# A two-block transformer forward pass on one core: PSUM reads of the latent attention moved to ScalarE, broadcast steps on VectorE, and three steps told or split earlier

## The chip, the cores and the metric

The kernel runs on one core of a Trainium2 chip. The metric is device time in microseconds (us); of the kernel before there are three runs.

## The reference, cut to what matters

All arithmetic is float32, 256 tokens of width 2048. A first block (sliding-window attention, gated linear attention, feed-forward, final norm) feeds a second one (convolution, latent attention, attention over 256 memory rows). Nearly all work is the product of activations with weights. What the change touches:

```python
q = (rms_norm(c_q, q_norm_g) @ w_uq).reshape(b, s, 16, 128 + 64)
q_nope = rms_norm(q[..., :128], qn_nope_g)
q_rope = apply_rope(rms_norm(q[..., 128:], qn_rope_g), cos, sin)
kv = (rms_norm(c_kv, kv_norm_g) @ w_ukv).reshape(b, s, 16, 128 + 128)
k_nope = rms_norm(kv[..., :128], kn_nope_g);  v = kv[..., 128:]
k_rope = apply_rope(rms_norm(k_rope_raw, kn_rope_g), cos, sin)
sc = q_nope @ k_nope + q_rope @ k_rope        # per head, masked by chunks of 64
o = softmax(sc * scale) @ v
k, v = split(rms_norm(mem, mem_norm_g) @ w_mem_kv)     # memory rows
x = rms_norm(x, norm_final_g)                # between the blocks; then normed again by block two
```

## The kernel before, in words

TensorE multiplies in float32 by three products: each weight is split into a high part `w_hi` (ScalarE, a copy to float32r, L1064) and a low part `w_lo` (VectorE, raw minus high, L1396); activations likewise. The unit of weights is a **granule**: 512 KB, 1024 columns, 12 matmuls of 128x512 (L437 to L439). SyncE loads granules into 8 raw buffers; the split parts have 4 buffers, so the split of granule g waits for granule g-4 to be used (`w_used`), and TensorE waits for `lo_done`. A **chunk** is a run of granules that fills one of two PSUM accumulators (`acc`); whoever reads it out tells `acc_free`. A **unit** is a small job of TensorE on one of four PSUM banks (transposes L568, scores L914 and L915, read-out L933): TensorE waits for `unit_src`, tells `unit_done`, and the reader tells `unit_free`. VectorE and ScalarE may also ask each other (`act_req`, `act_done`). Each engine runs its own list in the order written; a `Walk` object counts granules, chunks and units on ScalarE and VectorE, and `ahead`, `more`, `some`, `back` say at which place in the list a split stands.

**The latent attention** (16 heads, `mla_pair`, 8 pairs of heads, two loops i of four pr) takes two heads at once. TensorE: chunk `uq` (two granules of 768 columns), chunk `ukv` (two granules), then background chunks, cut into pieces by `MLA_BACK`: in even pairs `mz`, 8 granules, as 3, 2, 2, 1; in odd pairs `gc` and `conv_out`, 12 granules, as 4, 3, 3, 2. Between the pieces stand the pair's units: three of transposes (queries, rope queries, keys), two of scores, two transposing probabilities, one read-out. On VectorE a pair is: read `uq` (L2347) and `ukv` (L2354, L2357) from PSUM, twelve sums of squares (L1410), the reciprocal root by 11 small steps (`rsqrt`, L1416 to L1425), scale per head into `stage` (L2381, L2388, L2398), `rotate` the rope part, read the transposed units (L2403 to L2410), scale, mask and take the maximum of scores (L2422 to L2430), read the transposed probabilities (L2450), scale the read-out (L2463). ScalarE does the exponentials (L1143). The first pair of the first loop (`turn`) also turns half of the convolution. At pr 3 the next pair's four splits are not made ahead.

**The other places.** In four passes of the first block's feed-forward (`ffn_pass` with `mem`) TensorE also transposes a quarter of the raw memory rows behind the second granule of the `up` chunk (`with_turn`); VectorE tells `unit_src` for it at L1959, behind `take_silu`, though the rows lie in SBUF from the start. At the end of the feed-forward `square_parts` (L2050) takes for each of four quarters the sum of squares of x and of x times the gain, six VectorE instructions a quarter; quarters 2 and 3 stand between single splits. For the rope key (L2313 to L2322) VectorE norms and rotates 64 columns while `ckv` is multiplied.

## Time and profile before

| | us |
|---|---|
| three runs | 2757.66, 2759.08, 2759.46 (median 2759.08) |
| the profiled execution | 2757.25, span 2755.5 |
| TensorE busy, of the span | 2604.4 (95%) |
| VectorE busy | 1634.5 (59%) |
| ScalarE busy | 1082.2 (39%) |

The profile is one execution. Times in rows are us from the start of the span; PE is TensorE, DVE VectorE, ACT ScalarE. A bracket in a row of the timeline is the idle time before it and what ended it. "DVEq" is VectorE's queue: an increment of a semaphore, not an instruction's end.

### The profile page before, as it was taken

To read this page: it belongs to the slowest core of one execution; us is meant where nothing else is said; L and a number is where in the kernel's file an instruction comes from. 1 tells how busy PE (TensorE), PEld (TensorE's weight loads), DVE (VectorE), ACT (ScalarE), POOL (GpSimd) and SP (SyncE) were. 2 spreads that over 40 slices of the span, in tenths; PEclk is the share of its full clock that TensorE was granted. 3 is DMA by queue.
4 is the path that set the end of the run, shared out by engine and by line. 5 is a ranking of instruction groups with operands and counts; after the bars stand their busy time and mean duration, and the time that the engine had idled before them with its cause. 6 is when DMAs were issued, how large, how long until landed. Compare 5 with 4: busy or idle time off the path is not lost.

```text
span 2755.5 us, 31202 instructions
## 1 busy us (share of the span) xinstructions
PE 2604.4 (95%) x11745; PEld 2128.5 (77%) x11745; DVE 1634.5 (59%) x2588; ACT 1082.2 (39%) x1309; POOL 0.2 (0%) x4
## 2 busy tenths in 40 slices
PE   5999989999998999999999989899998998999999
PEld 4777667888877788888888768787887777778887
DVE  5565555456655555556556765557666767765454
ACT  3333423444433444433555434333333333334443
POOL 0000000000000000000000000000000000000000
PEclk9999999999999999999999999999999999999999
DMA  5855334655665566665656555455664444446554
GB/s 186 227 161 149 118 120 139 196 176 193 193 195 161 164 187 184 190 190 183 199 183 214 161 153 174 138 162 168 185 183 142 140 141 146 142 129 191 189 185 137
DMA packets 235304, 466.70 MB, mean 169 GB/s; under 512 B 19051, under 2 KB 27537, under 8 KB 234530
## 3 DMA queue, kind: packets, MB, share of 16 engines
q1 hardware_dynamic: 231296, 457.89, 53.3%
q10 hardware_dynamic: 3874, 7.01, 1.3%
q8 instruction: 85, 1.39, 0.2%
q14 instruction: 49, 0.40, 0.0%
HBM read 459.60 MB, written 5.24 MB: 169 GB/s over the span
## 4 chain that ended last, share of the span: by engine, by line
PE 85%; DVE 10%; DMA 2%; ACT 2%; issue 1%; SPq 0%; DVEq 0%; ACTq 0%
PE acc L437 24%; PE acc L439 23%; PE acc L438 23%; DVE w_lo L1396 2%; PE banks L568 2%; PE banks L774 1%; PE banks L773 1%; PE banks L775 1%; DMA bias_rows<-work 1%; PE acc L773 1%; PE acc L774 1%; PE acc L775 1%; ACT w_hi L1064 1%; DMA raw<-in_w_in_dram 1%; DVE etmp L1410 1%
## 5 line engine op out<-in xcount | busy, mean ns | idle before, releaser
L1396 DVE TENSOR_TENSOR w_lo<-raw,w_hi 128x1024 fp32r<-128x1024 f32 (+1 forms) x866 | 1042.9, 1219 | 857.4 <-ACT w_hi L1064 833.7
L1064 ACT ACTIVATE w_hi<-raw 128x1024 fp32r<-128x1024 f32 (+1 forms) x866 | 908.1, 1055 | 1357.8 <-PE acc L439 1220.8
L437 PE MATMUL acc<-w_hi,x_hi_A 128*128 128x512 f32 x1880 | 756.0, 402 | 28.6 <-DVE w_lo L1396 23.5
L438 PE MATMUL acc<-w_lo,x_hi_A 128*128 128x512 f32 x1880 | 741.3, 394 | 0.0
L439 PE MATMUL acc<-w_hi,x_lo_A 128*128 128x512 f32 x1880 | 741.2, 394 | 0.0
L437 PE MATMUL acc<-w_hi,x_hi_B 128*128 128x512 f32 (+1 forms) x1216 | 478.1, 393 | 11.1 <-DVE w_lo L1396 8.4
L438 PE MATMUL acc<-w_lo,x_hi_B 128*128 128x512 f32 (+1 forms) x1216 | 473.6, 389 | 0.0
L439 PE MATMUL acc<-w_hi,x_lo_B 128*128 128x512 f32 (+1 forms) x1216 | 473.5, 389 | 0.0
L437 PEld LDWEIGHTS acc<-w_hi,x_hi_A 128*128 128x128 f32 x1880 | 359.6, 191 | 113.6 <-issue 21.6
L439 PEld LDWEIGHTS acc<-w_hi,x_lo_A 128*128 128x128 f32 x1880 | 358.8, 191 | 77.4
L438 PEld LDWEIGHTS acc<-w_lo,x_hi_A 128*128 128x128 f32 x1880 | 359.9, 191 | 73.2 <-issue 0.8
L437 PEld LDWEIGHTS acc<-w_hi,x_hi_B 128*128 128x128 f32 x1216 | 231.1, 190 | 59.2 <-issue 10.6
L439 PEld LDWEIGHTS acc<-w_hi,x_lo_B 128*128 128x128 f32 x1216 | 230.6, 190 | 46.2
L438 PEld LDWEIGHTS acc<-w_lo,x_hi_B 128*128 128x128 f32 x1216 | 231.1, 190 | 44.4
L568 PE MATMUL banks<-cst,stage 128*128 128x128 f32 (+1 forms) x363 | 59.6, 300 | 66.1 <-DVE stage L1507 19.6
L568 PEld LDWEIGHTS banks<-cst,stage 128*128 128x128 f32 (+1 forms) x363 | 45.4, 152 | 81.0 <-DVE stage L1507 21.6
L773 PE MATMUL acc<-w_hi,x_hi_B 128*128 128x512 f32 x176 | 68.8, 391 | 0.9 <-DVE w_lo L1396 0.9
L775 PE MATMUL acc<-w_hi,x_lo_B 128*128 128x512 f32 x176 | 68.5, 389 | 0.0
L774 PE MATMUL acc<-w_lo,x_hi_B 128*128 128x512 f32 x176 | 68.5, 389 | 0.0
L773 PE MATMUL banks<-w_hi,x_hi_B 128*128 128x512 f32 x176 | 68.5, 389 | 0.0
L774 PE MATMUL banks<-w_lo,x_hi_B 128*128 128x512 f32 x176 | 68.5, 389 | 0.0
L775 PE MATMUL banks<-w_hi,x_lo_B 128*128 128x512 f32 x176 | 68.5, 389 | 0.0
(247 smaller groups left out, 1372.0 us busy)
## 6 DMA issues: line engine op xcount, KB each, us to landing
raw<-in_w_in_dram SPq DMA_DIRECT2D x377, 512.0 KB, 4.0
raw<-in_w_ffn_gate_dram SPq DMA_DIRECT2D x88, 512.0 KB, 4.3
raw<-in_w_ffn_up_dram SPq DMA_DIRECT2D x88, 512.0 KB, 4.4
raw<-in_w_ffn_down_dram SPq DMA_DIRECT2D x88, 512.0 KB, 4.4
raw<-in_w_out_dram SPq DMA_DIRECT2D x32, 512.0 KB, 4.4
raw<-in_w_mem_kv_dram SPq DMA_DIRECT2D x32, 512.0 KB, 4.7
raw<-in_w_mla_out_dram SPq DMA_DIRECT2D x32, 512.0 KB, 4.7
raw<-in_w_o_dram SPq DMA_DIRECT2D x32, 512.0 KB, 3.8
```

The source lines that it names most:

```text
L437: mm(o, xh, hi[:, k, :], start=(kt == first_k), stop=False)
L438: mm(o, xh, lo[:, k, :], start=False, stop=False)
L439: last = mm(o, xl, hi[:, k, :], start=False, stop=(kt == (last_k or c.kts) - 1))
L568: return pe.transpose(o, i, ident[0:i.shape[0], 0:i.shape[0]])
L773: mm(o[q][t], xh, hi, start=first, stop=False)
L774: mm(o[q][t], xh, lo, start=False, stop=False)
L775: ins = mm(o[q][t], xl, hi, start=False, stop=last)
L1064: act.activation(w_hi[:, s, 0:n], raw[:, r, 0:n], ACT.Copy).then_inc(hi_done, 1)
L1396: dve.tensor_tensor(w_lo[:, s, 0:n], raw[:, r, 0:n], w_hi32[:, s, 0:n], ALU.subtract).then_inc(lo_done, 1)
L1410: return dve.tensor_tensor_reduce(out=o, in0=a, in1=b, scale=1.0, scalar=0.0, op0=ALU.mult, op1=ALU.add, accum_out=acc_)
```

## The change

- Latent attention, ScalarE: it reads `uq`, `ukv` (a Square and a Copy of each part that is normed), the three transposed units and the two of probabilities. The split of ScalarE's list around them is as before.
- Latent attention, VectorE: sums of squares become three `tensor_reduce` over ScalarE's squares; the rope rotation is done on unscaled queries, before the first piece of background; the per-head scale becomes one `tensor_tensor` with a broadcast factor for each of three stage buffers; scores are scaled and masked in one step with a mask of three blocks; `rotate` takes both halves of the tokens at once. The order of the units becomes queries, keys, rope queries. Two units wait for `unit_free` (`taken`), since ScalarE now fills what they read.
- The next pair's four splits are made ahead at every pair but the last.
- Memory rows: `unit_src` is told at the head of the pass.
- Squares of quarters 2 and 3: ScalarE squares with a sum, VectorE multiplies the squares by the gain's squares (`fin_sq`, made once, at j = FG + 9) and sums: two instructions a quarter.
- Rope key: `W.more()`, two splits, ahead of it.

```diff
-            def unit(fill):
+            def unit(fill, taken=False):
                 pe.wait_ge(unit_src, U.at(1))
+                if taken:
+                    pe.wait_ge(unit_free, U.at())
...
+            for k in (2, 3):
+                for kt in (4 * k, 4 * k + 2):
+                    split_unit("A", kt, GCOL["norm_final_g"] + kt)
+                for t in range(T):
+                    ins = act.activation(squared[:, k - 2, t, :], xres[:, t, k * CW:(k + 1) * CW], ACT.Square,
+                                         accum_out=sm[:, 4 + 4 * t + k:5 + 4 * t + k])
+                ins.then_inc(squares_done, 1)
+                W.some(1)
...
+            def evac_unit(dst, n, scale=1.0):
+                act.wait_ge(unit_done, W.U.at(1))
+                act.activation(dst, W.bank()[:, 0:n], ACT.Copy, scale=scale).then_inc(unit_free, 1)
...
                 W.background(1 + pr % 2, False, 2)
+                act.wait_ge(w_used, W.E.next(uq.grans))
+                act.activation(q_squares, a[:, :, 0:384], ACT.Square)
+                act.activation(qs, a[:, :, 0:384], ACT.Copy).then_inc(release(uq), 1)
...
                 W.back(ks[0])
+                act.wait_ge(w_used, W.E.next(ukv.grans))
+                act.activation(k_squares, kv4[:, :, :, 0:DN], ACT.Square)
...
                 W.back(ks[1])
-                skip_units(3)
+                for dst, n, g in ((qnT, 512, "mla_qn_nope_g_2"), (knT, 512, "mla_kn_nope_g_2")):
+                    evac_unit(dst.rearrange("p h s -> p (h s)"), n, gcol[:, GCOL[g]:GCOL[g] + 1])
+                evac_unit(qrT, S)
...
-                if pr < 3:
+                if (i, pr) != (1, 3):
                     W.ahead(4)
...
             def ffn_pass(i, first=False, mem=None):
+                if mem is not None:
+                    for p in range(2):
+                        dve.sem_inc(unit_src, 1)
+                        SRC.n += 1
...
+                dve.wait_ge(*released(uq))
+                dve.tensor_reduce(sm[:, 4:8].rearrange(four, t=T), sq4[:, :, :, DN:DN + DR], AX.X, ALU.add)
+                dve.tensor_reduce(sm[:, 0:4].rearrange(four, t=T), sq4[:, :, :, 0:DN], AX.X, ALU.add)
...
+                rotate(rotated, rq, 2)
...
                 W.back(ks[0])
+                dve.wait_ge(*released(ukv))
+                dve.tensor_reduce(sm[:, 8:12].rearrange(four, t=T), k_squares, AX.X, ALU.add).then_inc(step, 1)
...
+                for u, (x, n, o) in enumerate(((q4[:, :, :, 0:DN], DN, 12), (kx, DN, 20), (rotated, DR, 16))):
...
+                    TT(s, x, r, ALU.mult).then_inc(unit_src, 3 if last else 1)
```

**How the order moves.** First place: VectorE, an even pair, from the reciprocal root (its last step) to the transposed units. `stage` is what TensorE transposes, `cs` the cosines, `banks` the units' PSUM. Before:

```order
L1425 SCALAR_TENSOR_TENSOR sm<-sm 128x12 [waits step]
L2381 TENSOR_SCALAR stage<-arena,sm 128x128 [waits step]
L2381 TENSOR_SCALAR stage<-arena,sm 128x128 x3
L2388 SCALAR_TENSOR_TENSOR arena<-arena,sm,rope_g 128x64 [waits unit_src]
L2388 SCALAR_TENSOR_TENSOR arena<-arena,sm,rope_g 128x64 x3
L2276 TENSOR_TENSOR stage<-arena,cs 128x2x32 [waits step]
```

and of the change:

```order
L1472 SCALAR_TENSOR_TENSOR sm<-sm 128x12 [waits step]
L2432 TENSOR_TENSOR stage<-arena,sm 128x512 [waits step]
L2432 TENSOR_TENSOR stage<-arena,sm 128x512 [waits unit_src]
L2432 TENSOR_TENSOR stage<-arena,sm 128x256 [waits unit_src]
L1443 TENSOR_TENSOR w_lo<-raw,w_hi 128x1024 [waits hi_done,unit_src]
L1443 TENSOR_TENSOR w_lo<-raw,w_hi 128x1024 [waits hi_done] x3
```

Behind the root there stood 24 instructions up to the last stage buffer, 12 of them the rotation; now there stand three.

Second place: ScalarE, from the second granule of background to the transposed units, of the change (before, only the L1074 rows were there, as L1064):

```order
L1383 ACTIVATE work<-acc 128x768 [waits w_used]
L1384 ACTIVATE arena<-acc 128x768
L1074 ACTIVATE w_hi<-raw 128x1024 [waits w_used,landed4]
L1074 ACTIVATE w_hi<-raw 128x1024 [waits w_used,landed5]
L1393 ACTIVATE work<-acc 128x512 [waits w_used]
L1394 ACTIVATE arena<-acc 128x512
L1395 ACTIVATE arena<-acc 128x512
L1074 ACTIVATE w_hi<-raw 128x1024 [waits w_used,landed6]
```

Five reads of PSUM now stand among the splits, each waiting for a chunk's end.

Third place: VectorE ahead of the rope key, of the change (before, the L1443 rows were absent here and came behind the rotation):

```order
L1541 SCALAR_TENSOR_TENSOR x_lo_B<-banks,gcol,x_hi_B 128x256
L1443 TENSOR_TENSOR w_lo<-raw,w_hi 128x1024 [waits hi_done,unit_free]
L1443 TENSOR_TENSOR w_lo<-raw,w_hi 128x1024 [waits hi_done]
L1457 ISA etmp,sm<-work 128x64
L1457 ISA sm 128x1
```

Two splits moved ahead of the key's norm. Activation tables are loaded seven times in either listing of ScalarE.

## Rows read from the trace of the kernel before

**Rows 1.** Waits of PE, whole span: us in total, times, longest

```profile
PE acc L437 <- DVE w_lo L1396: 31.9, 16, 4.3
PE banks L568 <- DVEq L1959: 14.6, 4, 3.7
PE banks L568 <- DVEq L2393: 12.9, 8, 2.2
```

**Rows 2.** Timeline of PE, feed-forward passes: start us, us, what

```profile
777.97 1.04 PE L568 MATMUL banks<-cst,stage 128*128 128x128 f32 x8
778.76 0.47 PE L437 MATMUL acc<-w_hi,x_hi_B 128*128 128x512 f32 x1
...
828.77 1.03 PE L568 MATMUL banks<-cst,stage 128*128 128x128 f32 x8
...
982.85 1.04 PE L568 MATMUL banks<-cst,stage 128*128 128x128 f32 x8
...
1027.26 1.03 PE L568 MATMUL banks<-cst,stage 128*128 128x128 f32 x8
```

**Rows 3.** Windows behind a restart: us, PE, PEld, DVE, ACT, POOL, PEclk, DMA, GB/s

```profile
2103.06:2109.06 6.00, 6.00 (x23) 4.93 (x22) 5.19 (x7) 1.06 (x1) 0.00 (x0) 0.79 0.74 235
2200.81:2206.81 6.00, 6.00 (x21) 4.83 (x20) 4.60 (x7) 1.06 (x1) 0.00 (x0) 0.68 0.72 234
2278.80:2284.80 6.00, 6.00 (x25) 6.00 (x26) 2.99 (x3) 1.06 (x1) 0.00 (x0) 0.72 0.85 277
1887.07:1893.07 6.00, 6.00 (x19) 4.81 (x20) 3.56 (x4) 1.06 (x1) 0.00 (x0) 0.72 0.80 276
1592.46:1598.46 6.00, 6.00 (x17) 4.77 (x18) 3.26 (x3) 0.80 (x1) 0.00 (x0) 0.62 0.82 265
```

**Rows 4.** Timeline of PE and DVE, squares of quarters 2 and 3

```profile
1579.92 0.47 PE L437 MATMUL acc<-w_hi,x_hi_A 128*128 128x512 f32 x1 [0.94 <-DVE w_lo L1396]
...
1585.11 0.50 PE L437 MATMUL acc<-w_hi,x_hi_A 128*128 128x512 f32 x1 [2.19 <-DVE w_lo L1396]
...
1592.46 0.76 PE L437 MATMUL acc<-w_hi,x_hi_A 128*128 128x512 f32 x1 [4.33 <-DVE w_lo L1396]
...
1574.40 0.69 DVE L1410 CUSTOM_DVE_ANT_0 etmp<-xres 128x512 f32<-128x512 f32 x1
```

**Rows 5.** Timeline of PE and DVE, the rope key

```profile
1887.07 0.73 PE L437 MATMUL acc<-w_hi,x_hi_A 128*128 128x512 f32 x1 [4.35 <-DVE w_lo L1396]
...
1880.70 0.22 DVE L1410 CUSTOM_DVE_ANT_0 etmp<-work 128x64 f32<-128x64 f32 x1
...
1885.79 4.63 DVE L1396 TENSOR_TENSOR w_lo<-raw,w_hi 128x1024 fp32r<-128x1024 f32 x4
```

**Rows 6.** Timeline of PE, latent attention, around the three transposed units

```profile
2094.34 0.39 PE L439 MATMUL acc<-w_hi,x_lo_A 128*128 128x512 f32 x1
...
2144.76 0.60 PE L568 MATMUL banks<-cst,stage 128*128 128x128 f32 x4
...
2148.68 0.50 PE L437 MATMUL acc<-w_hi,x_hi_A 128*128 128x512 f32 x1 [0.60 <-DVE w_lo L1396]
...
2194.43 0.39 PE L439 MATMUL acc<-w_hi,x_lo_A 128*128 128x512 f32 x1
...
2278.80 0.41 PE L437 MATMUL acc<-w_hi,x_hi_B 128*128 128x384 f32 x1 [3.48 <-DVE w_lo L1396]
```

**Rows 7.** Durations: by line and shape (busy us, mean ns), and DVE's timeline

```profile
L1075 ACT ACTIVATE x_hi_B<-banks 128x512 fp32r<-128x512 f32 x20 | 12.0, 598 | 67.4 <-PE banks L568 66.2 <-DVEq L1478 1.3
L1064 ACT ACTIVATE w_hi<-raw 128x768 fp32r<-128x768 f32 x16 | 13.0, 838 | 10.7 <-PE acc L439 10.7
L2210 DVE TENSOR_TENSOR work<-banks,work 128x512 f32<-128x512 f32 x4 | 2.8, 690 | 0.1
...
2095.29 0.17 DVE L1416 TENSOR_SCALAR sm<-sm 128x12 f32<-128x12 f32 x1
...
2097.55 0.88 DVE L2381 TENSOR_SCALAR stage<-arena,sm 128x128 f32<-128x128 f32 x4
```

More of the change, by code:

```diff
@@ L917, in fill @@
                         return last
-                    unit(fill)
+                    unit(fill, taken=(h == 0))
                 back(ks[2])
@@ L935, in fill @@
                     return last
-                unit(fill)
+                unit(fill, taken=True)
             for k in range(4):
@@ L2086, in _ @@
                     square_parts(j - FG - 7)
+                if j == FG + 9:
+                    TT(fin_sq, fin_g[:, 2 * CW:], fin_g[:, 2 * CW:], ALU.mult).then_inc(step, 1)
+                    dve.wait_ge(step, V.next())
             def add_part(k):
@@ L2108, in _ @@
                 W.some(1)
-                square_parts(k)
+                dve.wait_ge(squares_done, k - 1)
+                for t in range(T):
+                    ins = ttr(squared[:, k - 2, t, :], squared[:, k - 2, t, :], fin_sq[:, (k - 2) * CW:(k - 1) * CW],
+                              sm[:, 12 + 4 * t + k:13 + 4 * t + k])
+            ins.then_inc(step, 1)
+            dve.wait_ge(step, V.next())
             W.some(1)
@@ L2366, in mla_pair @@
                 W.back(ks[0])
-                for t in range(T):
-                    for h in range(2):
-                        for q, (x, n, o) in enumerate(((qs[:, t, h * 192:h * 192 + DN], DN, 0),
-                                                       (qs[:, t, h * 192 + DN:(h + 1) * 192], DR, 4), (kx[:, t, h, :], DN, 8))):
-                            k = 6 * t + 3 * h + q
-                            ins = ttr(squares[:, k, 0:n], x, x, sm[:, o + 2 * t + h:o + 2 * t + h + 1])
-                ins.then_inc(step, 1)
@@ L2382, in mla_pair @@
-                ins.then_inc(unit_src, 1)
-                dve.wait_ge(unit_src, SRC.next())
-                s2 = stage[:, W.U.slot(4, 1), 0:256].rearrange("p (t h n) -> p t h n", t=T, h=2)
-                rq = rop[:, 1:3, :].rearrange("p t (h n) -> p t h n", h=2)
-                for t in range(T):
-                    for h in range(2):
-                        ins = STT(rq[:, t, h, :], qs[:, t, h * 192 + DN:(h + 1) * 192], sm[:, 16 + 2 * t + h:17 + 2 * t + h],
-                                  rope_g[:, 0, :], ALU.mult, ALU.mult)
@@ L2390, in mla_pair @@
-                ins.then_inc(step, 1)
-                dve.wait_ge(step, V.next())
-                rotate(s2, rq, 2)
-                dve.sem_inc(unit_src, 1)
-                SRC.n += 1
-                s = stage[:, W.U.slot(4, 2), :].rearrange("p (t n) -> p t n", t=T)
-                for t in range(T):
-                    for h in range(2):
-                        ins = TS(s[:, t, h * DN:(h + 1) * DN], kx[:, t, h, :], sm[:, 20 + 2 * t + h:21 + 2 * t + h], None, ALU.mult)
-                ins.then_inc(unit_src, 1)
@@ new lines, in mla_pair @@
+                for u, (x, n, o) in enumerate(((q4[:, :, :, 0:DN], DN, 12), (kx, DN, 20), (rotated, DR, 16))):
+                    s = stage[:, W.U.slot(4, u), 0:4 * n].rearrange("p (t h n) -> p t h n", t=T, h=2)
+                    r = sm[:, o:o + 4].rearrange(four, t=T).unsqueeze(3).to_broadcast([P, T, 2, n])
+                    last = u == 2
+                    TT(s, x, r, ALU.mult).then_inc(unit_src, 3 if last else 1)
+                    dve.wait_ge(unit_src, SRC.next(3 if last else 1))
@@ L2417, in mla_pair @@
+                W.back(ks[1])
+                W.U.next(3)
                 W.back(ks[2])
@@ L2447, in mla_pair @@
                 dve.wait_ge(step, V.next())
-                for h in range(2):
-                    dve.wait_ge(unit_done, W.U.at(1))
-                    CP(work[:, 1024 + h * 384:1024 + (h + 1) * 384], W.bank()[:, 0:384]).then_inc(unit_free, 1)
-                    dve.wait_ge(unit_free, W.U.next())
-                dve.sem_inc(unit_src, 1)
-                SRC.n += 1
-                if pr < 3:
+                W.U.next(2)
+                if (i, pr) != (1, 3):
                     W.ahead(4)
```

154 lines of the change are left out of this document (67 added, 87 removed).

## The prediction, as written before the run

> **What bounds the kernel now.** I read the page first: TensorE is busy for 95% of the span, VectorE 59%, ScalarE 39%. So time can only be won where TensorE waits, or where its clock is low behind a wait. The list of its waits comes next [rows 1]: 31.9 us for the low half of a weight in 16 waits, 14.6 us in four waits for the semaphore increment of L1959 (the memory rows), 12.9 us in eight waits for L2393 (the rope transposes). Each of these names a place of the change, so I followed TensorE's timeline at each, and the list of windows for the clock behind it [rows 3]. What the reader is to see there: in the 6 us behind a restart at 2103.06 the granted clock was 0.79, at 2200.81 0.68, at 2278.80 0.72, at 1887.07 0.72, at 1592.46 0.62. With the clock c, TensorE loses (1 - c) times 6 us: 1.26, 1.92, 1.68, 1.68 and 2.28 us. These restarts stand behind single waits of 3.5 us or more, or behind a row of shorter ones that hold it up for over 5 us; the waits of 0.94 and 2.19 us [rows 4] cost nothing of the kind, since the matmul rows behind 1585.11 have their usual spacing. A removed long wait is therefore worth its length and some 1.3 to 2.3 us more.
>
> The sum is made against the profiled execution, 2757.25 us, which is 1.8 us below the median of the three runs, 2759.08.
>
> **Memory rows, four passes.** Before, VectorE tells TensorE only when it has finished the gate of the pass, though the rows have long been in SBUF. A pass with memory rows lasts 828.77 - 777.97 = 50.80 us, one without 1027.26 - 982.85 = 44.41 us [rows 2]. Of the 6.39 us between them 0.79 is the work of eight more transposes (777.97 to 778.76 shows what eight take), 5.6 is waiting and what follows it; 14.6 / 4 = 3.7 of it is the named wait [rows 1]. Told at the head of the pass, the unit finds its source and ScalarE's and VectorE's reads of it come earlier, behind which nothing new stands. Gain 4 x 5.6 = 22.4 us. The least is the named wait alone, 14.6, if the rest of the difference comes from reading the units out.
>
> **Squares of quarters 2 and 3.** TensorE waits 0.94, 2.19 and 4.33 us here for low halves [rows 4], which stand in VectorE's list behind twelve instructions of about 0.69 us. Four of 0.69 are left: 8 x 0.69 = 5.5 us less ahead of the last split. ScalarE's squares hold up its second pair of turned tiles by about 0.6, so the restart of 1592.46 comes 4.9 us earlier; about 3.3 us of some 7.5 of waiting stay, shorter pieces, and a quarter of the 2.28 us of low clock goes with them: 5.5 us in all. Bounds: 3 (ScalarE's four squares on the path, 4 x 0.6 [rows 7]) and 7.5 + 2.3 = 9.8 (all of it gone).
>
> **Rope key.** Its norm and rotation hold VectorE from 1880.70 to 1885.79, 5.1 us, ahead of the four splits of 4.63 us, and TensorE waits 4.35 us and restarts at 0.72 [rows 3, 5]. With two splits ahead of it TensorE has two granules to work on. A granule is 12 matmuls, and by 512 columns the rows stand 0.227 us apart, so 2.72 us; two give 5.4, two splits take 2.3 and the key 5.1, so the third low half is late by 5.1 + 1.16 - 5.4 + 0.2, about 1.1 us. Gain 4.35 - 1.1 + 1.68 = 5.0. Bounds 3.3 (the clock stays low) and 6.0.
>
> **Latent attention.** Here lies most. The stretch from the last matmul of a piece to the restart holds ten transposes, 1.0 us of work. In an even pair it is 2200.81 - 2194.43 = 6.38 us [rows 3, 6]; less 0.23 for the last matmul and 1.0 it is 5.15 of waiting, with 1.92 of clock 7.1; three such pairs, 21.2. In an odd pair 2148.68 - 2144.76 = 3.92, less 1.0, is 2.9 us with the full clock; four, 11.7.
>
> Does the new chain end in time? Let E be the end of chunk `ukv` on TensorE. ScalarE first makes one split, 1.06 [rows 3], then reads three times 512 columns at 0.60 [rows 7]: E + 2.9. VectorE's reduction of 512 columns is taken like its other steps of that size, 0.69, then a small step, then the root's eleven steps, 2097.55 - 2095.29 = 2.26, then the first stage buffer, one step of 0.69 [rows 7]: E + 6.8. TensorE has three granules in between and comes at E + 8.2, in odd pairs, with four, at E + 10.9. All three buffers stand at E + 8.0, and behind them the splits follow at once, where rotation and twelve more steps stood. So the stretch shrinks to its transposes, with 1.4 us to spare in even pairs and 4.1 in odd ones. The banks are read by ScalarE, which is idle around that point.
>
> The Trainium skill (VectorE: DVE Perf Modes, "The perf-mode tier table (the rule you actually need)") speaks against one step: in float32 from SBUF a tensor_scalar runs at twice the rate of a tensor_tensor, so that one broadcast TENSOR_TENSOR in place of four TENSOR_SCALARs should be the dearer. Here four of L2381 took 0.88 us and one TENSOR_TENSOR over the same 512 columns 0.69 [rows 7]: at 128 columns the fixed part outweighs the rate. By the rule without a fixed part the step would cost twice the four, 1.76, and the sum would fall by the first pair's 1.1 us alone, since 1.1 fits the 1.4 of slack.
>
> The first pair is held up by the turned convolution too, which stays; TensorE stands from 2094.34 [rows 6]. From the root's end, 2097.55, to the restart at 2103.06 there are 5.5 us; now three steps of 0.69 overlapped with transposes, 2.2: 3.3 less, and about 1.0 from the sums of squares, 4.3; some 4.5 with the low clock stays. Between the two loops, at 2278.80, a wait of 3.48 and 1.68 of clock goes, since the next pair's splits are made ahead: 5.2. Together 21.2 + 11.7 + 4.3 + 5.2 = 42.4 us.
>
> What is added: ScalarE's reads, per pair two of 768 columns (0.84), five of 512, and shorter ones, some 6.0 us, 48 in all; its list has that room (39% busy), and TensorE doesn't wait for ScalarE as long as no split is behind time. VectorE loses its PSUM reads and most of the 24 steps. No DMA is added. Lowest value for this term: 18.1, if only the rope wait (12.9 [rows 1]) and the one between the loops (5.2) go and the rest turns into late splits; highest 42.4 + 4.5, if the first pair stops waiting too.
>
> **Sum.** 22.4 + 5.5 + 5.0 + 42.4 = 75.3. 2757.25 - 75.3 = 2681.95; for a median 1.8 more, 2683.8, so **2684.0 us** in round numbers. With the edges of the parts that I trust least (5 us either way on the memory rows and the first pair, 5 on the clock) its own band is 2676 to 2692.
>
> **Rivals.** *ScalarE comes late in the latent attention.* It works in order, and its reads stand among splits that TensorE needs, each read waiting for a chunk's end. The slack in even pairs is 1.4 us, by estimates; a semaphore's way of 0.2 us at each of five handovers eats 1.0 of it, and at the pair's end the next four splits stand behind two reads of the probabilities. If it is gone, TensorE waits some 1.5 us in each of eight places and loses clock at some: + 16, so 2700. For it speaks that the order gives it no way to pass a read that waits; against it, that ScalarE was idle 10.7 us for TensorE ahead of the sixteen splits of 768 columns alone [rows 7], so it runs ahead of TensorE there. Chance 0.13. *The memory wait moves.* The unit's banks, or the splits behind the gate, may be what the pass really waits for; then the named 14.6 us turn up under another releaser, and of 22.4 nothing is won: 2706. Against it: nothing in the pass stands between the rows and the transposes but VectorE's order. Chance 0.07. *The low clock stays.* If the restarts are behind many short waits that still hold the clock down, of the clock's share (5.8 + 1.7 + 1.7 + 0.6 = 9.8, and up to 2 more in the memory passes) nothing comes back: about 2695. The 0.94 and 2.19 us waits speak against it. Chance 0.06. *Slower.* ScalarE's in-order list becomes the bound of the whole latent attention: every one of its 48 us of new reads delays a split that TensorE waits for, and the old waits stay in new names. That would be 2757.25 - 32.9 + 48 + 1.8, about 2774. It decides once a pair's reads and splits exceed the pair's time, about 50 us (2144.76 to 2194.43 [rows 6]); 6 us and up to 16 splits of 1.06 come to half of that, so 0.02. *The change does not do what it says.* The activation tables would be reloaded with each Square between Copies, at TensorE's cost; the order lists seven loads before and after, so I give it no chance of its own.
>
> **How the numbers follow.** Forecast 0.72, the rivals 0.13, 0.07, 0.06 and 0.02. The predicted time is the forecast's, 2684.0. The range is 2676 to 2706: from the lower edge of the forecast's band over the first three rivals; what is left out is the slower rival and the tails. A measurement of this kernel can tell 0.2%, 5.5 us, from no change. Faster by more than that: all but the last rival and a mixture of several misses, 0.97; within it 0.01; slower 0.02.
>
> **What the profile after should show.** The wait for the memory rows' increment is gone from TensorE's list, and passes with them last 45.2 us. In the stretch of the squares one wait of about 3 us is left. At the rope key a wait of about 1 us with full clock. In pairs two to eight no wait of more than 0.3 us at the transposes, and windows of 6 us behind them at a clock of 0.95 or more; the first pair keeps about 3 us. VectorE's share falls by some 3 points, ScalarE's rises by 2. I am wrong if the waits for `w_hi` or for `unit_free` appear on TensorE in the latent attention, if the releaser of the transposes is ScalarE, or if a pass with memory rows still lasts over 48 us.

## The result, and the profile after

| | before | the change |
|---|---|---|
| median of four runs, us | 2758.97 | 2682.5 (2679.47 to 2685.19) |
| ratio, 95% interval | | 0.9723 (0.9706 to 0.974) |
| the profiled execution, us | 2757.25 | 2679.47, span 2677.7 |
| TensorE busy | 2604.4 (95%) | 2579.6 (96%) |
| VectorE busy | 1634.5 (59%) | 1567.6 (59%) |
| ScalarE busy | 1082.2 (39%) | 1123.5 (42%) |

The change is faster by 76.5 us, 2.8%. The forecast was 2684.0 us in a range of 2676 to 2706, with 0.97 for faster.

TensorE's list of waits now begins as follows (us in total, times, longest):

```profile
PE banks L578 <- DVE stage L1554: 18.6, 6, 15.2
PE acc L444 <- DVE w_lo L1443: 17.0, 8, 5.3
...
PE banks L578 <- DVE stage L2204: 10.0, 4, 4.0
...
PE banks L578 <- DVE stage L2432: 1.8, 1, 1.8
```

The reader is to see what is missing. The increment ahead of the memory rows (14.6 us) and the rope transposes' (12.9 us) of [rows 1] have no line any more, and of the 31.9 us for low halves in 16 waits 17.0 in 8 are left. The three steps that fill the latent attention's stage buffers, L2432, are waited for once in eight pairs. L1554 is the start of the kernel, L2204 a place that the change does not touch.

To see where the time was won I laid the two traces beside each other by the running number of the accumulating matmul (the same matmul of the program in both) and read off how much earlier it starts. The differences between two such points are the gains of a stage:

| stage | predicted | the two traces |
|---|---|---|
| start to the first memory pass | 0 | 0.3 (up to 1.6 either way in between) |
| four passes with memory rows | 22.4 | 21.9 |
| squares of quarters 2 and 3 | 5.5 | 7.8 |
| rope key | 5.0 | 5.1 |
| latent attention: first pair | 4.3 | 5.6 |
| three more even pairs | 21.2 | 20.2 |
| four odd pairs | 11.7 | 11.7 |
| between the loops | 5.2 | 5.3 |
| all other places | 0 | -0.1 |
| sum | 75.3 | 77.8 |

### The profile page after: what moved, and what is told of

It is laid out like the page before. It is cut to its first block, busy times and chain, and to the rows that moved or that the text cites. A ratio compares the mean times of both kernels' runs of the same rounds, so it can differ in the third digit from the quotient of the medians.

```text
span 2677.7 us, 30783 instructions
## 1 busy us (share of the span) xinstructions
PE 2579.6 (96%) x11745; PEld 2115.2 (79%) x11745; DVE 1567.6 (59%) x2198; ACT 1123.5 (42%) x1397; POOL 0.2 (0%) x4
## 4 chain that ended last, share of the span: by engine, by line
PE 66%; DVE 4%; ACT 1%; issue 1%; DVEq 0%; ACTq 0%
PE acc L444 18%; PE acc L446 18%; PE acc L445 18%; PE banks L578 2%; PE banks L785 1%; PE banks L783 1%; PE banks L784 1%; PE acc L783 1%; PE acc L785 1%; PE acc L784 1%; DVE w_lo L1443 1%; PE banks L925 1%; PE banks L924 1%; ACT w_hi L1074 1%; DVE etmp L1457 0%
## 5 line engine op out<-in xcount | busy, mean ns | idle before, releaser
L1443 DVE TENSOR_TENSOR w_lo<-raw,w_hi 128x1024 fp32r<-128x1024 f32 (+1 forms) x866 | 1043.1, 1218 | 888.5 <-ACT w_hi L1074 866.2
L1074 ACT ACTIVATE w_hi<-raw 128x1024 fp32r<-128x1024 f32 (+1 forms) x866 | 906.6, 1054 | 1214.1 <-PE acc L446 1081.1
```

The costliest lines, as they stand in the source:

```text
L1074: act.activation(w_hi[:, s, 0:n], raw[:, r, 0:n], ACT.Copy).then_inc(hi_done, 1)
L1443: dve.tensor_tensor(w_lo[:, s, 0:n], raw[:, r, 0:n], w_hi32[:, s, 0:n], ALU.subtract).then_inc(lo_done, 1)
```

## The steps in the new profile

The passes with memory rows, TensorE's timeline of the change. The first two rows are the heads of two passes with memory rows, the last two of passes without:

```profile
777.63 1.04 PE L578 MATMUL banks<-cst,stage 128*128 128x128 f32 x8
...
822.97 1.04 PE L578 MATMUL banks<-cst,stage 128*128 128x128 f32 x8
...
960.62 1.04 PE L578 MATMUL banks<-cst,stage 128*128 128x128 f32 x8
...
1005.07 1.03 PE L578 MATMUL banks<-cst,stage 128*128 128x128 f32 x8
```

A pass with memory rows takes 45.34 us, where [rows 2] had 50.80, and one without 44.45. The difference of 0.89 is the work of eight more transposes; nothing of the waiting is left.

The squares and the rope key, the only waits that TensorE has in these stretches (bracket: idle time before):

```profile
1564.21 0.47 PE L444 MATMUL acc<-w_hi,x_hi_A 128*128 128x512 f32 x1 [2.32 <-DVE w_lo L1443]
...
1859.06 0.47 PE L444 MATMUL acc<-w_hi,x_hi_A 128*128 128x512 f32 x1 [0.89 <-DVE w_lo L1443]
```

Of three waits of 7.46 us in [rows 4] one of 2.32 is left; of the 4.35 of [rows 5], 0.89 (the prediction said about 3.3 and 1.1).

The second even pair, VectorE's timeline and then TensorE's, from the keys' squares to the restart:

```profile
2145.72 0.69 DVE L2424 TENSOR_REDUCE sm<-work 128x4 f32<-128x512 f32 x1
...
2148.50 0.17 DVE L1472 SCALAR_TENSOR_TENSOR sm<-sm 128x12 f32<-128x12 f32 x1
2148.70 1.95 DVE L2432 TENSOR_TENSOR stage<-arena,sm 128x512 f32<-128x512 f32 x3
...
2151.08 1.25 PE L578 MATMUL banks<-cst,stage 128*128 128x128 f32 x10
2152.09 0.48 PE L444 MATMUL acc<-w_hi,x_hi_A 128*128 128x512 f32 x1
```

The ten transposes stand in one row without a bracket and take 1.01 us up to the restart. In [rows 6] the same work and its waits took 6.38, counted from the last matmul ahead of it; counted in the same way it is now 1.24 (0.23 for that matmul). The first buffer is filled from 2148.70 to about 2149.4, and TensorE comes at 2151.08: 1.7 us to spare. The prediction had reckoned 1.4.

Windows of 6 us behind restarts (PE, PEld, DVE, ACT, POOL busy, PEclk, DMA share, GB/s): behind the one wait left at the squares, the rope key, the second even pair and between the loops, and then two of those that wait as before:

```profile
1564.21:1570.21 6.00, 6.00 (x26) 4.96 (x27) 4.49 (x4) 1.26 (x2) 0.00 (x0) 1.00 0.78 260
1859.06:1865.06 6.00, 6.00 (x26) 4.96 (x27) 5.93 (x9) 1.51 (x3) 0.00 (x0) 1.00 0.85 285
2150.85:2156.85 6.00, 6.00 (x33) 5.10 (x32) 3.91 (x4) 3.55 (x5) 0.00 (x0) 1.00 0.62 189
2220.17:2226.17 6.00, 6.00 (x40) 5.91 (x39) 4.44 (x7) 2.12 (x2) 0.00 (x0) 1.00 0.84 288
...
2402.69:2408.69 6.00, 6.00 (x19) 4.78 (x20) 3.49 (x4) 1.06 (x1) 0.00 (x0) 0.72 0.82 266
2043.62:2049.62 6.00, 6.00 (x19) 4.81 (x20) 5.93 (x13) 0.54 (x1) 0.00 (x0) 0.72 0.85 280
```

Where the wait went, the clock is at its full level, 2.4 GHz, against the 0.62 to 0.79 of [rows 3]. Behind the 3.80 us that stay at the last pair's end it is still 0.72, a mixture of both levels (2.4 and 1.2 GHz) within the 6 us.

## The experiments

Twelve kernels ran, each four times, with the kernel before on the same chip (medians 2757.2 to 2759.9). Ratios are to that one. Between executions of one kernel the time mostly scatters by 3 us either way (4.5 in the widest cases), so medians settle differences of 5 us and more, and for smaller ones the traces are laid beside each other as above, over the stage in question alone. The theory: TensorE's waits were set by VectorE's order and the length of its chains, each part of the change is worth its own waits and the clock behind them, and in the latent attention all comes down to one slack.

### One part alone: the memory rows

On the kernel before:

```diff
             def ffn_pass(i, first=False, mem=None):
+                if mem is not None:
+                    for p in range(2):
+                        dve.sem_inc(unit_src, 1)
+                        SRC.n += 1
                 W.split_next()
                 take_silu(hid, gate_c)
                 if mem is not None:
                     for p in range(2):
-                        dve.sem_inc(unit_src, 1)
-                        SRC.n += 1
                         ask_high()
```

> The kernel before with one part of the change alone: the memory rows are told at the head of the pass. My theory (VectorE's order alone held the unit back, 5.6 us a pass): 22.4 us faster than before, about 2736.6, and passes with memory rows at 45.2 us; the two traces so far show 21.9 for this stretch. Rival (the wait only moves to another releaser, and the gain needs the rest of the change): under 8 us faster, 2751 or more, with a new releaser for some 14 us.

2738.89 us (2734.87 to 2741.01), ratio 0.9931 (0.9914 to 0.9947). By the medians this is 18.3 us, less than the 22.4 expected. The traces tell more: over the four passes this one is 21.9 us faster than before, as the change is (21.9), and the execution had lost 5.1 us ahead of them, at places that no part of the change touches. The heads of the passes stand at 783.03, 828.37, 873.71 and 919.05, so 45.34 apart. No new releaser came up. The part does its work alone; the rival falls. Of the 21.9 us 14.6 are the named wait. The rest is the low clock that stood behind it in the kernel before; this is the window behind the first of the four waits:

```profile
788.15:794.15 6.00, 6.00 (x24) 5.21 (x25) 1.38 (x2) 0.48 (x1) 0.00 (x0) 0.72 0.32 88
```

That is (1 - 0.72) x 6 = 1.7 us a pass, 6.7 in four.

### Squares undone

```diff
-            for k in (2, 3):
-                for kt in (4 * k, 4 * k + 2):
-                    split_unit("A", kt, GCOL["norm_final_g"] + kt)
-                for t in range(T):
-                    ins = act.activation(squared[:, k - 2, t, :], xres[:, t, k * CW:(k + 1) * CW], ACT.Square,
...
+            for kt in range(8, KT, 2):
+                split_unit("A", kt, GCOL["norm_final_g"] + kt)
...
-                dve.wait_ge(squares_done, k - 1)
...
+                square_parts(k)
```

> The changed kernel with quarters 2 and 3 squared on VectorE again, as before. My theory, with what the two traces show for this stretch (7.3 us where I had predicted 5.5): 7 us slower than the change, about 2689.5, with waits of 0.9, 2.2 and 4.3 us and a window of low clock back. Rival (the predicted size was right and the rest is the clock's scatter between two executions): 5.5 us or less, 2688 or less, and the clock in the 6 us behind the last wait stays at 1.00.

2688.81 us (2687.95 to 2693.31), ratio 0.9756 (0.974 to 0.9772); over the stage 7.3 us slower than the change. TensorE's timeline with its waits, and the windows behind the second and third:

```profile
1559.04 0.47 PE L443 MATMUL acc<-w_hi,x_hi_A 128*128 128x512 f32 x1 [0.95 <-DVE w_lo L1436]
1564.23 0.50 PE L443 MATMUL acc<-w_hi,x_hi_A 128*128 128x512 f32 x1 [2.19 <-DVE w_lo L1436]
1571.57 0.48 PE L443 MATMUL acc<-w_hi,x_hi_A 128*128 128x512 f32 x1 [2.73 <-DVE w_lo L1436]
```

```profile
1564.23:1570.23 6.00, 4.61 (x12) 3.13 (x12) 4.93 (x32) 1.06 (x1) 0.00 (x0) 0.72 0.30 87
1571.57:1577.57 6.00, 6.00 (x19) 4.78 (x20) 3.41 (x4) 1.06 (x1) 0.00 (x0) 0.72 0.80 258
```

The third wait is 2.73 us, where before it was 4.33 [rows 4]. The restarts at 1564.23 and 1571.57 are 7.34 us apart, before 7.35 (1585.11 and 1592.46): VectorE's chain sets the time, and whether TensorE goes through its granule at 0.72 and waits 2.73, or goes at full clock and waits 4.33, comes to the same. **A low clock ahead of a wait is free where the chain that ends the wait doesn't itself wait for TensorE; the one behind the last wait is paid.** So a gain is read off the restarts, not off the waits. The condition matters: ahead of the first pair of the latent attention the chain hangs on TensorE's granules, and there a low clock is not free, as the next run and the convolution's splits show.

The expectation had a third wait of 4.3 us and the window back at a low clock; the second came, the first only in this disguise. The rival, that the clock is partly a matter of the execution, isn't wholly out either. In nine of eleven kernels with the new squares the clock behind the wait of 2.32 us was 1.00. In two it was not (the splits between the loops undone, and the convolution's splits ahead, both below), and there the stage gained 6.3 us and not 7.8:

```profile
1564.08:1570.08 6.00, 6.00 (x20) 4.86 (x21) 3.46 (x4) 1.26 (x2) 0.00 (x0) 0.72 0.82 263
```

### The rope key's two splits undone

```diff
                 low_part("B", 8 + 2 * p, GCOL["mla_q_norm_g_2"] + 2 * p)
-            W.more()
```

> The changed kernel without the two splits ahead of the rope key's norm. My theory: the wait of 4.35 us and 1.7 us of low clock come back for 0.89 us: 5 us slower than the change, about 2687.5. Rival (rotation in fewer steps had already shortened VectorE's stretch, so that part of the gain isn't the two splits'): 3.5 us or less, since rotating both halves at once saves some 0.8 us of it.

2691.64 us (2684.47 to 2693.15), ratio 0.9764 (0.9748 to 0.978). The median is 9 us above the change's, but its scatter is the widest of all; over the stage the trace is 4.7 us slower. The wait is 3.92 us and the clock behind it 0.72:

```profile
1858.41:1864.41 6.00, 6.00 (x19) 4.79 (x20) 3.55 (x4) 1.06 (x1) 0.00 (x0) 0.72 0.79 259
```

3.92 is 0.43 less than the 4.35 of [rows 5]: so much the merged rotation saves here, the rest is the two splits'. The theory holds, and the rival has a small share.

The traces show one thing more. Behind the wait of 2.02 us ahead of the latent attention this kernel has a clock of 1.00, the change 0.72 (rows in the last section). Counted from the same matmul ahead of that wait, the first pair's restart comes 1.6 us later in the change, though both wait 1.83 us at the transposes: VectorE's chain there waits for TensorE itself (in the change 1.83 us for the turned tiles, up to 2051.49). So of the 4.7 us that the two splits give at the rope key the change lost 1.6 again, and 3.1 are left by the traces. Whether the splits bring that low clock with them stays open.

### The splits between the loops undone

```diff
-                if (i, pr) != (1, 3):
+                if pr < 3:
                     W.ahead(4)
```

(and `W.ahead(4)` at the head of each loop's first pair again, on both engines.)

> The changed kernel with the splits between the two loops over the pairs made late again, as before (three pairs of four make them ahead). My theory: the wait of 3.5 us and 1.7 us of low clock between the loops come back, 5.2 us slower, about 2687.7. Rival (with the read-out behind ScalarE's new reads the late splits cost more, or the clock part is not paid): 3.5 us, or over 7 us.

2688.18 us (2685.31 to 2690.26), ratio 0.9746 (0.973 to 0.9762). The wait is back with 3.54 us, the window behind it at 0.72, and over the stage the trace is 5.3 us slower. As expected.

### The latent attention's slack: four ways to lengthen the chain

VectorE's work on the queries behind the keys' read:

```diff
-                dve.tensor_reduce(sm[:, 4:8].rearrange(four, t=T), sq4[:, :, :, DN:DN + DR], AX.X, ALU.add)
...
-                rotate(rotated, rq, 2)
...
                 W.back(ks[0])
                 dve.wait_ge(*released(ukv))
+                dve.tensor_reduce(sm[:, 4:8].rearrange(four, t=T), sq4[:, :, :, DN:DN + DR], AX.X, ALU.add)
...
+                rotate(rotated, rq, 2)
```

> The changed kernel with VectorE's work on the queries (two reductions, the gain, the rotation) moved behind the read of the keys and values, where it stood before. In the trace of the change this block takes 2.9 us (2140.35 to 2143.21), and the first stage buffer is ready 1.7 us before TensorE comes in an even pair, 4.4 us in an odd one. My theory (slack decides): even pairs two to four wait 1.2 us each, odd ones nothing, the first pair 2.9 less what its conversion work hides, some 2: 5 to 6 us slower than the change, about 2688, or 3 to 5 more if the clock falls behind these waits. Rival (the whole gain is ScalarE's reads; the place of the block does not matter): no difference. Rival (the splits behind the block come late too): over 15 us.

More reads on ScalarE (4, and in another kernel 2):

```diff
+                for _ in range(4):
+                    act.activation(k_squares, kv4[:, :, :, 0:DN], ACT.Square).then_inc(again, 1)
+                    act.wait_ge(again, AG.next())
                 act.activation(k_squares, kv4[:, :, :, 0:DN], ACT.Square)
```

> The changed kernel with four more Squares of 512 columns on ScalarE ahead of the keys' one, each waiting for the one before; their results are overwritten by the same values. Some 0.7 us each, 2.8 us a pair, on the chain to the stage buffers. My theory (1.7 us of slack in even pairs): 1.1 us of waiting in each of three pairs, 2.8 in the first, some 6 us slower, about 2688.5. Rival of the prediction (ScalarE's list is near its bound, splits come late as well): more than 15 us slower, with low halves of weights or w_hi as releasers.

> The changed kernel with two more Squares of 512 columns on ScalarE ahead of the keys' one (four more took 2.47 us and made even pairs two to four wait 0.74 us each, which leaves 1.73 of slack). Theory of the slack as a threshold: 1.24 us is under 1.73, so no wait in pairs two to eight; the first pair, which has none, waits 1.24 longer; median within 2 us of the change. Rival (each added read costs its share, 1.24 us x 8 = 10): 2692.

The keys and values read by VectorE again, and their squares summed there:

```diff
-                act.activation(k_squares, kv4[:, :, :, 0:DN], ACT.Square)
...
+                TS(kvv.rearrange("p t (h n) -> p t h n", h=2), kv4[:, :, :, DN:256], 0.5, None, ALU.mult).then_inc(step, 1)
...
+                CP(kz, kv4[:, :, :, 0:DN]).then_inc(acc_free[W.C.slot(2, -1)], 1)
...
-                dve.tensor_reduce(sm[:, 8:12].rearrange(four, t=T), k_squares, AX.X, ALU.add).then_inc(step, 1)
+                        ins = ttr(k_squares[:, t, h, :], kz[:, t, h, :], kz[:, t, h, :], sm[:, 8 + 2 * t + h:9 + 2 * t + h])
```

> The changed kernel, but VectorE reads the keys and values from PSUM again (two steps) and sums the keys' squares itself (four steps), while ScalarE keeps the queries, the turned units and the probabilities. In the trace of the change VectorE is done with its splits at 2145.61, ScalarE with these reads at 2145.69: they only lie beside each other. On VectorE's own list the chain grows by 2 x 0.69 + 4 x 0.21 less 0.69 for the reduction, about 1.6 us with the handovers, just under the slack of 1.73. Theory of the slack: no wait, or one under 0.2 us, in pairs two to eight, the first pair 1.6 us more; median within 3 us of the change. Rival (ScalarE's read of the keys is what made the latent attention faster): waits of over 1 us in even pairs and waits in odd ones, 2690 or more.

What they measured (waits at the three transposed units):

| kernel | chain longer by | first pair's wait | pairs 3, 5, 7 | odd pairs | median, us | ratio |
|---|---|---|---|---|---|---|
| the change | 0 | 1.83 | 0 | 0 | 2682.5 | 0.9723 |
| two Squares more | 1.24 | 3.08 | 0 | 0 | 2684.53 | 0.9731 (0.9714 to 0.9748) |
| keys on VectorE | 1.6 | 3.40 | 0 | 0 | 2685.2 | 0.9727 (0.9711 to 0.9744) |
| four Squares more | 2.47 | 4.36 | 0.74 | 0 | 2688.76 | 0.9751 (0.9735 to 0.9767) |
| queries late | 2.9 | 4.74 | 1.13 | 0 | 2692.92 | 0.9764 (0.9747 to 0.978) |

Here "pairs 3, 5, 7" are the even pairs of the program but the first. The row of the four Squares on ScalarE's timeline, and TensorE's wait and restart:

```profile
2147.53 2.47 ACT L1396 ACTIVATE work<-acc 128x512 f32<-128x512 f32 x4
```

```profile
2155.38 1.69 PE L579 MATMUL banks<-cst,stage 128*128 128x128 f32 x10 [0.75 <-DVE stage L2437]
2156.83 0.48 PE L445 MATMUL acc<-w_hi,x_hi_A 128*128 128x512 f32 x1
```

The first pair, which has no slack, waits longer by 1.25, 1.57, 2.53 and 2.91 us: the length of what was added, whichever engine it was added to. The even pairs take 1.7 us of it for nothing (2.47 - 0.74 = 1.73, 2.9 - 1.13 = 1.77), the odd ones all. That is a threshold for the first buffer, as the kernels with 1.24 and 1.6 us show. A pair that does wait loses more than the wait: the transposes then go at the pace of the three stage buffers, 1.45 us up to the restart (2155.38 to 2156.83) against 1.01. With the granted clock at 1.00 in that window an even pair came to 1.35 us for a wait of 0.74, and 1.7 for one of 1.13. The threshold isn't quite sharp, since the second and third buffer come later than the first. With the keys on VectorE TensorE doesn't wait for the first one, but the ten transposes take 1.32 us in even pairs:

```profile
2156.01 1.56 PE L578 MATMUL banks<-cst,stage 128*128 128x128 f32 x10
2157.33 0.48 PE L444 MATMUL acc<-w_hi,x_hi_A 128*128 128x512 f32 x1
```

Two Squares more make it 1.09. Both medians are beside the change's within the scatter. So ScalarE's read of the keys alone bought 0.3 us in each of three even pairs, nothing in the four odd ones, and its 1.6 us in the first pair; it is the sum of the parts that brings the chain under the granules. No run here takes back alone ScalarE's reads of the queries, of the turned units or of the probabilities, or the rotation ahead of the root, so how the 42.8 us divide between them stays open.

Two expectations were too low for the queries put late: the first pair waits the whole 2.91 us longer and not "some 2", and the clock behind it is at 0.72, which the expectation had as its upper case (10.4 us slower by the medians).

No wait for `w_hi` or for a bank came up on TensorE in any of them, also with 8 x 2.47 us more on ScalarE. The rival "ScalarE comes late" falls, as far as 8.5 us a pair.

### Four scaling steps in place of a broadcast

```diff
-                    TT(s, x, r, ALU.mult).then_inc(unit_src, 3 if last else 1)
+                    for t in range(T):
+                        for h in range(2):
+                            ins = TS(s[:, t, h, :], x[:, t, h, :], sm[:, o + 2 * t + h:o + 2 * t + h + 1], None, ALU.mult)
+                    ins.then_inc(unit_src, 3 if last else 1)
```

> The changed kernel with each of the three broadcast TENSOR_TENSORs split into four TENSOR_SCALARs of 128 or 64 columns, as before the change. My theory (4 x 0.22 = 0.88 against 0.69, twice, and about 0.6 against 0.4): 0.6 us more in all, inside the slack of even pairs; the first pair waits 0.2 to 0.6 longer; time the same within 0.1%. Rival (TENSOR_SCALAR runs at a higher rate, so the broadcast is dearer): the stage buffers stand earlier than in the change and the first pair's wait of 1.83 us shrinks.

2682.06 us (2679.65 to 2686.33), ratio 0.9726 (0.971 to 0.9742): the same. The first pair waits 2.02 us for the first buffer, not 1.83, and 0.25 more for the next. So the broadcast is the cheaper by about 0.2 us a buffer at this size (16 of them took 692 ns each), and no gain of TENSOR_SCALAR's rate shows.

### Further on: three more places

The last pair's four splits ahead as well:

```diff
                 if (i, pr) != (1, 3):
                     W.ahead(4)
+                else:
+                    W.split_next()
...
-            W.split_next()
```

> The changed kernel, but the four splits behind the last pair are made ahead too. It is meant to beat both. The wait of 3.80 us at 2402.69 and the low clock behind it (0.72 over 6 us, 1.7 us) go, as they did between the loops: 5.5 us faster than the change, about 2677. Rival (the splits ahead of the last sum delay the read-out, which TensorE then waits for): nothing, or up to 4 us slower.

2676.18 us (2672.83 to 2676.56), ratio 0.9698 (0.9682 to 0.9714). The wait of 3.80 us is gone, the window at 2400 to 2406 has a clock of 1.00, and over the stage the trace is 5.7 us faster than the change. As expected.

Then the splits behind the convolution's second half, ahead of its last product and copies:

```diff
+                if h == 1:
+                    W.ahead(2)
                 TT(bgt, bgt, etmp[:], ALU.mult).then_inc(step, 1)
...
-                if turn:
-                    W.ahead(2)
```

> The kernel with the last pair's splits ahead, and VectorE's two splits behind the second half of the convolution made ahead of its last product and its two copies to the stage buffers (2.1 us). The wait of 2.02 us at 2043.62 goes, with the low clock behind it, which one execution in two showed (0.72 in 6 us, 1.7 us, or none): 2 to 3.7 us faster than with the last pair alone (2676.2), about 2673.5. Rival (the first pair's chain is held by the convolution's turned tiles, so what is won ahead is waited for at its transposes): the wait of 1.83 us grows by as much and nothing is won.

2676.33 us (2674.14 to 2678.66), ratio 0.9703 (0.9684 to 0.9721): nothing won in the median. The wait of 2.02 us is gone from its place, but another of 2.00 comes up two granules ahead of the first pair's transposes. The first two rows are of this kernel, the third of the change:

```profile
2055.84 0.50 PE L444 MATMUL acc<-w_hi,x_hi_A 128*128 128x512 f32 x1 [2.00 <-DVE w_lo L1444]
...
2060.68 1.69 PE L578 MATMUL banks<-cst,stage 128*128 128x128 f32 x10 [1.83 <-DVE stage L2433]
...
2062.14 1.69 PE L578 MATMUL banks<-cst,stage 128*128 128x128 f32 x10 [1.83 <-DVE stage L2432]
```

VectorE can't begin the split that is waited for here until the turned tiles of the convolution are read, back and forth with ScalarE, from 2050.03 to 2054.55; the change had this from 2051.49. The wait at the transposes is 1.83 us as before; the rival had it grow there, and not two granules ahead.

What was won shows at the restart behind the transposes, counted from the same matmul ahead of the wait of 2.02 us. It comes 1.8 us sooner than in the change, but only 0.2 sooner than in the kernel with the rope key's splits undone, which had the full clock behind that wait. So of 2 us won ahead 1.8 are waited for, and the rival was right in that; 1.6 are the low clock that the change had there. They are lost again at once, since now the clock behind the transposes is low, where the change had 1.00. The first row is of this kernel, the second of the change:

```profile
2060.68:2066.68 6.00, 5.92 (x23) 4.63 (x24) 4.60 (x5) 1.65 (x3) 0.00 (x0) 0.72 0.39 97
2062.14:2068.14 6.00, 5.93 (x30) 4.81 (x31) 4.95 (x6) 2.71 (x4) 0.00 (x0) 1.00 0.40 117
```

The next kernel, with the same splits, shows the same: the restart 1.8 us sooner, then 0.72.

And in the attention over the memory rows the change's broadcast step in a new place:

```diff
-                for t in range(T):
-                    for hh in range(2):
-                        TS(qx[:, t, hh * ED:(hh + 1) * ED], qx[:, t, hh * ED:(hh + 1) * ED], sm[:, 4 + 2 * t + hh:5 + 2 * t + hh], None, ALU.mult).then_inc(step, 1)
-                        dve.wait_ge(step, V.next())
+                rr = sm[:, 36:40].rearrange("p (t h) -> p t h", t=T)
+                CP(sm[:, 36:40], sm[:, 4:8]).then_inc(step, 1)
+                dve.wait_ge(step, V.next())
                 for hh in range(2):
-                    CP(W.slot().rearrange("p (t n) -> p t n", t=T), qx[:, :, hh * ED:(hh + 1) * ED]).then_inc(unit_src, 1)
+                    TT(W.slot().rearrange("p (t n) -> p t n", t=T), qx[:, :, hh * ED:(hh + 1) * ED],
+                       rr[:, :, hh:hh + 1].to_broadcast([P, T, ED]), ALU.mult).then_inc(unit_src, 1)
```

> That kernel, and in the attention over the memory rows the queries' per-head scale is written straight into the stage buffers by one broadcast TENSOR_TENSOR a head, in place of four scaling steps and two copies. Ahead of the first unit stood 1.52 + 0.43 us, now 0.2 + 0.69: the two waits of 4.05 us at this place become 3.0, two of 0.93 change little: 2 us faster, about 2671.5; the clock behind the waits stays low. Rival (the unit is bound by something else than VectorE's chain): same time as with the convolution's splits ahead.

2670.49 us (2669.9 to 2673.35), ratio 0.9681 (0.9664 to 0.9699). The two waits of 4.05 us are 2.96 and 2.97, those of 0.93 are 1.17:

```profile
1595.45 1.12 PE L578 MATMUL banks<-cst,stage 128*128 128x128 f32 x4 [2.96 <-DVE stage L2204]
```

That explains some 2 us; the traces show about 3 over the two places with the clock behind them, and 1.6 more at the squares, where the kernel compared with had the low clock and this one 1.00. The 5.8 between the medians is more, so the rest is scatter. This kernel beats both: 12 us under the change.

## Why the prediction was right

**What bounds it.** The gain came from TensorE's waits and the clock behind them, and from nothing else: TensorE's idle time at rows with a wait fell from 135.1 to 81.7 us (summed over its timeline, without the first wait of all, for a DMA), that is 53.4 of the 77.8 between the two profiled executions. The rest is matmuls that no longer run at the low clock (granted over the whole span: 0.980 before, 0.991 now), and single matmuls' spacing behind restarts.

**Memory rows, 22.4 against 21.9.** Right as worked out, and shown alone. The low end, the named 14.6 us only, was too careful: the rest of the difference was the same wait's as well, by way of the clock (0.72 behind each, 6.7 us).

**Squares, 5.5 against 7.8.** The mechanism held, the size did not. The term that was mis-sized is the clock's: the prediction gives back "a quarter of the 2.28 us of low clock", 0.6, and measured are 2.1, since the window behind the restart at 1564.21 has 1.00. That restart came 5.7 us earlier where 4.9 was reckoned. The prediction's figures don't agree with each other here: 4.9 us off 7.5 of waiting leave 2.6 and not "about 3.3"; left were 2.32. The clock's part was in part luck, since two of eleven kernels had 0.72 behind the same wait and gained 6.3 us there.

**Rope key, 5.0 against 5.1.** Wait 0.89 where 1.1 was forecast, and the full clock behind it. The run without the two splits gives them 4.7 of it and the merged rotation 0.4, which the prediction had not counted.

**Latent attention, 42.4 against 42.8.** Pairs and the place between the loops came within 0.7 us each of what was said, the chain ended 1.7 us ahead instead of 1.4, and the four runs on the slack show that this number decides in even pairs. The first pair gave 5.6, not 4.3. Three things are in it that the prediction didn't have. The chain is shorter by more than was reckoned: where the clock ahead is the same as before (the run with the rope key's splits undone) the restart comes 6.0 us earlier, not 4.3 (a wait of 0.94 us at 2091.69 is gone too). Behind the restart the clock is 1.00, where it was 0.79, which gives 1.2; the prediction had left the low clock standing there. And in the change a low clock behind the wait of 2.02 us, which the kernel before did not have, takes 1.6 back. So 6.0 + 1.2 - 1.6 = 5.6: the nearness to 4.3 is in part luck. That the three buffers end some 1.2 us after the first ("All three buffers stand at E + 8.0" against E + 6.8) also tells why a pair that is late loses 0.6 us beside its wait.

**The rule of the page.** The Trainium skill (VectorE: DVE Perf Modes, "The perf-mode tier table (the rule you actually need)") would have the tensor_scalar at twice the rate of the tensor_tensor in float32. The table is for single instructions of 2048 columns. Here, at 128 columns a step, four TENSOR_SCALARs came out 0.2 us dearer than the one TENSOR_TENSOR of 692 ns. That doesn't speak against the table, which no run here can test at its size; it shows that steps this short are not where that rate counts.

**The rivals.** ScalarE did not come late; with 2.47 us more a pair it did not either. The memory wait did not move. In this execution the low clock went wherever the wait went, but came up anew behind the wait of 2.02 us. The slower case fell with the first of these. One of the argument's supports was wrong: that a wait of about 2 us costs no clock. It was true of the rows it was read from (0.92 behind the wait of 2.19 us at 1585.11), but the same wait has 0.72 in the kernel with the squares undone. On it hung the low chance of the rival "the low clock stays"; that rival did not come true as a whole, but a share of the clock's gain goes with the execution, as the squares show.

**The signs that were named.** All that the prediction listed for the profile came, but one: VectorE's share of the span was to fall by some 3 points and fell by 0.8 (59.3% to 58.5%), since its busy time went down by 67 us only and the span became shorter too. ScalarE's rose by 2.7, where 2 were said.

## What to carry to other kernels

Where one engine feeds another in order, look for the chain that ends last and count its slack in the consumer's own work: parts under the slack are all but free, whichever engine has them, and those over it cost at least their length, and may bring the low clock behind. Read gains off the restarts and not off the waits, since a low clock ahead of a wait is paid by the wait, unless the chain that ends the wait hangs on the slowed engine itself. And a semaphore that is told later than its data are ready is the cheapest thing to mend: 22 of 78 us came from two lines moved.

## What the runs showed of the hardware

A wait of TensorE of some 2 us may have the low clock behind it or not. Ahead of the latent attention TensorE waits 2.02 us in every kernel here but the two with the convolution's splits ahead. The window behind it in the kernel before, and in the change without the rope key's splits:

```profile
2078.66:2084.66 6.00, 6.00 (x28) 4.96 (x29) 4.45 (x5) 0.00 (x0) 0.00 (x0) 1.00 0.76 243
```

```profile
2050.03:2056.03 6.00, 6.00 (x29) 4.98 (x30) 5.93 (x13) 0.54 (x1) 0.00 (x0) 1.00 0.82 263
```

and in the change itself (0.72, the window of 2043.62 above) and without its squares:

```profile
2052.17:2058.17 6.00, 6.00 (x19) 4.79 (x20) 5.93 (x13) 0.55 (x1) 0.00 (x0) 0.72 0.81 260
```

So 0.28 x 6 = 1.7 us come or go at such a place. Here it need not be chance. The clock was 1.00 in all three kernels without the rope key's splits ahead (the one before, the memory rows alone, the key's splits undone) and 0.72 in all nine with them. In those three the rope key's wait has the low clock behind it, in the nine it has not. With one profile a kernel, that this is the cause is not shown.

At other places it does differ between executions of the same instructions. In the change a wait of 1.55 us had 1.00 behind it, and the same wait in the kernel with the squares undone, which up to there is the same program, 0.72:

```profile
170.42:176.42 6.00, 6.00 (x31) 4.99 (x32) 3.50 (x9) 2.48 (x11) 0.00 (x0) 1.00 0.29 90
```

```profile
171.11:177.11 6.00, 6.00 (x24) 4.83 (x25) 3.51 (x9) 2.35 (x11) 0.00 (x0) 0.72 0.31 90
```

Of the 14 traces four have 1.00 here. Over the first 350 us two executions differ by up to 5.7 us, in this way and by the length of the first waits. That is a large part of the scatter of the medians, and why stages were compared here and not only totals. The length of the wait alone doesn't tell which it will be: a wait of 3.08 us (first pair, two Squares more) had 1.00 behind it,

```profile
2063.78:2069.78 6.00, 5.93 (x30) 4.79 (x31) 4.94 (x6) 2.71 (x4) 0.00 (x0) 1.00 0.38 110
```

while one of 2.7 us between the attention over the memory rows and the rope key (at 1757.50 in the change) had 0.72 in every trace. What tips it stays open. Behind waits of 3.4 us and more the clock was low in every trace (0.50 to 0.74), but for the first waits at the kernel's start: behind 15.29 us the kernel before had 1.00.

```profile
27.15:33.15 6.00, 4.02 (x20) 3.21 (x20) 4.59 (x13) 3.36 (x8) 0.00 (x0) 1.00 0.00 0
```
